# Second layer's mixer: two links of the memory cells' gate chain beside each step of the attention

## The reference, cut to what matters

```python
att_x = window_attention(q, k, v, k_ctx, v_ctx, sink_g)      # 8 heads, softmax with a sink
qk = silu(depthwise_conv(concat([qm, km]), conv_w, conv_b))  # queries and keys of the memory cells
g  = GATE_CAP * tanh((gt + b_gates) / GATE_CAP)              # 16 gate rows: input and forget, forward and backward
lf = log_sigmoid(f_pre);  b = cumsum(lf);  ig = i_pre        # the gate chain, for 4 heads, both directions
m_t = maximum(b + m, running max of (ig - b) + b)            # a running maximum keeps the exponentials bounded
h  = (weights exp(..) of b, ig, m_t) applied to v            # the memory cells (mlstm), forward and backward
out = concat([rmsnorm(att), headnorm(h) * sigmoid(om)]) @ w_out
```

## Time and profile before

| | us |
|---|---|
| median of three runs | 2580.0 |
| the profiled execution's own time | 2587.1 |
| its span | 2585.3 |
| TensorE busy (96% of the span) | 2479.1 |
| VectorE busy (70%) | 1821.8 |
| ScalarE busy (51%) | 1313.2 |

### The profile page before, as it was taken

The page is one execution under the profiler, slowest core; times in us unless marked ns, Lnnn a source line. Parts: engine busy times, 40 slices in busy tenths (PEclk is TensorE's granted clock), DMA queues, the critical chain, the costliest instruction groups (busy, mean ns, idle before and its releaser), DMA issues.

```text
span 2585.3 us, 33643 instructions
## 1 busy us (share of the span) xinstructions
PE 2479.1 (96%) x13301; PEld 2005.1 (78%) x13301; DVE 1821.8 (70%) x2874; ACT 1313.2 (51%) x1992; POOL 66.3 (3%) x71
## 2 busy tenths in 40 slices
PE   7999999999999988999999999999998999998998
PEld 2564657788886667878778788787898999988998
DVE  6777627676432554989889889898876775675774
ACT  3135523222232543878767777777644554545543
POOL 0000000000010000000000000000000000000000
PEclk8999999999999988999999999999999999999999
DMA  7522024555312103989879889898743345433552
GB/s 284 224 99 81 1 82 165 193 203 187 130 50 82 66 1 127 361 312 369 308 300 364 311 335 344 314 368 317 280 165 113 142 170 206 152 130 115 177 182 98
DMA packets 71679, 511.03 MB, mean 198 GB/s; under 512 B 7905, under 2 KB 9057, under 8 KB 10049
## 3 DMA queue, kind: packets, MB, share of 16 engines
q1 hardware_dynamic: 68690, 500.21, 52.2%
q10 hardware_dynamic: 2208, 6.32, 0.7%
q0 software_dynamic: 592, 1.97, 0.2%
HBM read 506.23 MB, written 2.23 MB: 197 GB/s over the span
## 4 chain that ended last, share of the span: by engine, by line
PE 84%; DVE 8%; ACT 4%; issue 1%; DMA 1%; POOL 0%; DVEq 0%; ACTq 0%
PE bank L804 83%; DVE UL L2074 2%; ACT UH L1592 1%; DVE arena L2082 1%; ACT arena L1595 1%; PE bank L1176 1%; DMA consts<-in_c 1%; DVE arena L2074 1%; DVE XT L2082 1%; DVE JUNK L2121 0%; DVE arena L2078 0%; ACT XT L1595 0%; DVE small L2141 0%; ACT L1595 0%; DVE arena L2774 0%
## 5 line engine op out<-in xcount | busy, mean ns | idle before, releaser
L2074 DVE TENSOR_TENSOR UL<-ring,UH 128x1024 fp32r<-128x1024 f32 (+1 forms) x804 | 970.3, 1217 | 359.4 <-ACT UH L1592 339.7
L1592 ACT CAST UH<-ring 128x1024 fp32r<-128x1024 f32 (+1 forms) x804 | 830.1, 1040 | 603.2 <-PE bank L804 582.2
L804 PE MATMUL bank<-UH,HGh 128*128 128x512 f32 (+1 forms) x768 | 294.8, 384 | 21.4 <-DVE SCx L2078 16.4
L804 PE MATMUL bank<-XH,UH 128*128 128x256 f32 x1040 | 303.2, 292 | 5.0 <-DVE UL L2074 3.9
L804 PE MATMUL bank<-XL,UH 128*128 128x256 f32 x1040 | 294.6, 283 | 0.0
L804 PE MATMUL bank<-XH,UL 128*128 128x256 f32 x1040 | 294.6, 283 | 0.0
L804 PE MATMUL bank<-UH,HGl 128*128 128x512 f32 (+1 forms) x768 | 291.1, 379 | 0.5 <-issue 0.5
L804 PE MATMUL bank<-UL,HGh 128*128 128x512 f32 (+1 forms) x768 | 290.0, 378 | 0.0
L804 PE MATMUL bank<-arena 128*64 128x256 f32 (+7 forms) x856 | 201.3, 377 | 15.6 <-ACT arena L1592 6.4
L2121 DVE CUSTOM_DVE_ANT_0 JUNK<-ring,CROW 128x1024 bf16<-128x1024 f32 x176 | 206.3, 1217 | 13.9 <-ACT CROW L1595 10.0
L804 PEld LDWEIGHTS bank<-XH,UH 128*128 128x128 f32 x1040 | 199.4, 192 | 14.7 <-issue 6.5
(11 more groups left out here) (216 smaller groups left out, 4022.4 us busy)
## 6 DMA issues: line engine op xcount, KB each, us to landing
ring<-in_w SPq DMA_DIRECT2D x477, 1024.0 KB, 4.9
XT<-in_x ACTq DMA_DIRECT2D x2, 1024.0 KB, 12.1
bias_scratch<-BIAS POOLq DMA_DIRECT2D x6, 192.0 KB, 2.1
consts<-in_c ACTq DMA_DIRECT2D x1, 1109.0 KB, 8.2
out_y<-XT ACTq DMA_DIRECT2D x2, 512.0 KB, 3.5
BIAS<-bias_scratch POOLq DMA_DIRECT2D x1, 768.0 KB, 6.9
constd<-in_c ACTq DMA_DIRECT2D x1, 768.0 KB, 4.1
consts<-in_c ACTq DMA_DIRECT2D x1, 512.0 KB, 17.6
```

The costliest lines, as they stand in the source:

```text
L804: return e.matmul(out, lhsT, rhs, start=start, stop=stop, skip_group_check=True)
L1592: return e.copy(out, in_)
L2074: return e.tensor_tensor(out, a, b, op)
```

## The change

In layer `l`, `l + 1` links follow each step of the attention in the place of one. Layer 0 keeps one, and its list is the same as before. In layer 1 two follow each:

```diff
+        def more():
+            for _ in range(min(l + 1, len(rest))):
+                out.append(("rest", l, rest.pop(0)))
+
         def beside(with_rest):
             acc[0] += ATT_RATE[l]
             while acc[0] >= 1:
@@
-                    if with_rest and rest:
-                        out.append(("rest", l, rest.pop(0)))
+                    if with_rest:
+                        more()
@@
         while i_att[0] < n_att:
             out.append(("att", l, i_att[0]))
             i_att[0] += 1
-            if rest:
-                out.append(("rest", l, rest.pop(0)))
+            more()
```

## The result

The changed kernel takes 2565.1 us (median of four runs, 2560.5 to 2567.7) against 2582.4 for the kernel before in the same set of runs (2577.1 to 2587.5). The ratio is 0.9932, 95% interval 0.9909 to 0.9955: 17.4 us faster by the medians, 12 to 24 by the interval. The forecast was 11 us. The profiled execution took 2567.7 us, its span 2565.9.

A forecast was written before the change was run, and what follows sets the result against it. TensorE was taken to bound the kernel, with removable gaps in the second layer's mixer tail. The terms 9.3 + 1.8 = 11.1 us took 2580.0 to 2569 us; range 2560 to 2579.

The forecast's parts named there:

- Under the projections: Second layer's projections beside the attention: VectorE and ScalarE come late, mostly covered by vm projections; 0.5 us of TensorE stall.
- Table loads: The ln and its two table loads move from the tail to att 8, under om and vm, costing nothing there.
- The chain behind the attention: Second layer's tail: links behind the attention move earlier; memory starts 15.0 us earlier at full clock, 9.3 with it down.
- The new wait for em: Second layer's tail: TensorE, done with values 11 at 904.0, waits 0.6 us for ScalarE's em at 904.6.
- The clock: Second layer's tail: one fall of TensorE's clock, low from about 906, leaving memory's start 9.3 us earlier.
- The start of `memory`: First matmuls of memory, before at half clock, give back 1.8 us; bounds 0 and 2.4.
- The rival of the full clock: Second layer's tail: the clock stays full, gaining 15.0 + 1.8 = 16.8 us, to 2563 us; chance 0.23.

The follow-up runs named there:

- both_layers: Changed kernel with two links of the chain per attention step in the first layer too; ratio 0.9995 against the kernel before.
- before_no_ln: Kernel before with the second layer's logarithm replaced by an equally long exponential, leaving out two table loads; mixer stretch 213.2 us against 217.4, ratio 0.9980.
- after_no_ln: Changed kernel with the second layer's logarithm replaced by an equally long exponential, leaving out two table loads; mixer stretch 201.0 us against 202.6.
- back_only: Second layer's links placed one per attention step up to att 11, two from att 12 on; ratio 0.9966 against the kernel before.
- fill: Changed kernel plus four useless 384-column matmuls ahead of each of the second layer's two small-matmul groups; ratio 0.9932 against the kernel before.
- split: Changed kernel with the second layer's links reordered so the two small-matmul groups stand apart; ratios 0.9922 and 0.9936 against the kernel before.
- three: Changed kernel with three links per attention step in the second layer instead of two; ratio 0.9953 against the kernel before.
- again: Changed kernel once more, unaltered; ratio 0.9942 against the kernel before.

## Why the prediction was right, and where it was off

The direction, the place and the kind of every priced step held, and one term was mis-sized, the length of the clock's fall. The new wait of 0.95 us for ScalarE in the tail was not in the forecast; it cost nothing, being hidden by the wait for em.

- *Under the projections.* I gave 0.5 us of stall; there was none. VectorE came to share 3 at 850.6 (850.2 forecast), exponential 5 ran at 852.5 (852.2), convs ended at 858.6, the clear at 862.1, and exponential 6 at 861.6 with its reading. The waits of VectorE and ScalarE were as long as forecast, and the vm projections covered them. `both_layers` shows TensorE waiting where VectorE and ScalarE come late and the cover is less.
- *Table loads.* Those of the ln left the tail, where they had cost 4.2 us (`before_no_ln`), and cost nothing under the projections (`after_no_ln`).
- *The chain behind the attention.* The stretch of 12.5 us is gone; what is left of it in the tail is TensorE's own part, the small matmuls at 3.15 us in the place of 5.28. `back_only` without the first half of the move has 6.8 of 14.8.
- *The new wait for em.* 0.6 forecast, 0.38 measured, with em ending at 904.6 in either, on a trace that is 0.8 later.
- *The clock.* The lean to one fall in the tail was right, and `fill`, `split`, `back_only` and `three` show the small matmuls to be its cause. Its length was the mis-sized term. I took the clock as low from 906 until the last values were done, so that `memory` would start 9.3 us earlier. It was low from about 907 to 914: values 13 took 3.68 us but values 15 1.94. `memory` started 12.1 us earlier on the trace, 13.0 without the offset, where the forecast had 9.3. These 3.7 us are all of the difference between the mixer's gain (14.8) and the forecast (11.1). By the forecast's own times 2.9 of them are the clock: 1.2 up to the start of values 15 (914.75 against 915.9) and 1.7 in values 15. The other 0.8 is em, which ended at 904.6 on a trace that is 0.8 later; 0.5 of it would be the stall under the projections that did not come.
- *The start of `memory`.* 1.8 us given, 1.8 measured (13.0 of the 14.8 lie ahead of it).
- The rival of the full clock, 16.8 us, is what `fill` and `split` reached, with lists of their own: 17.0 and 17.9 us of S.

The median's further 2.6 us (17.4 against 14.8) are not shown to be the change's: `again` has 13.1 in total with the same list, and both intervals hold 14.8. The range of 2560 to 2579 held the time, 2565.1. That the median lies as far below the forecast of 2569 as it does is in part the luck of this set of runs.

## What to carry to other kernels

Look for a serial chain that stands behind the stage in which its engines idle, and move it under the stretch in which the bounding engine has ready work of its own; how many links go with each step is bounded by the slack of the shared queues, as the same move in a layer whose VectorE was 98% busy in places gave the whole gain back. Then look at what the moved work does to the clock: here it paid to keep the two groups of four-column matmuls apart (3 us of S). Judge such an edit by a stretch between two events of the trace, as the total varied by more than the difference between good lists.

## What the runs showed of the hardware

A group of four-column matmuls was followed by a fall of TensorE's clock also where TensorE had no wait right ahead of it and was busy all through it. In `three` 24 records of them, 3.01 us with values of the attention before and a projection behind, were followed by a clock of 0.62 from 892 to 895. In `back_only` the same 24, 2.84 us right behind values 15, which had waited 0.68 us before they started, were followed by 0.50 from 921 to 924. The two stretches:

```profile
892.00:895.00 3.00, 3.00 (x10) 2.40 (x10) 0.00 (x0) 0.00 (x0) 0.00 (x0) 0.62 0.03 5
```
```profile
921.00:924.00 3.00, 3.00 (x8) 2.37 (x8) 1.18 (x4) 2.08 (x7) 0.55 (x1) 0.50 0.00 0
```

In groups of 1.95 and 0.95 us with attention between them they left the clock at 1.00 (`split`). The Trainium skill ("TensorE: Matmul & The Clock Gate", What's actually happening) says that the gate follows how busy TensorE has been. With the profile's busy time as the measure the two stretches above do not bear that out: TensorE was busy in all of both and in the groups ahead of them.
